# Two of every eight pairs of K tiles in the up projection by seven block products, in groups of 1024 columns

## The reference

```python
D_MODEL = 2048
D_FF = 4 * D_MODEL
...
hn = rmsnorm(h, mlp_norm[l])
u = jnp.square(jax.nn.relu(hn @ w_up[l]))
h = h + u @ w_down[l]
...
return rmsnorm(h, final_norm)
```

## Time and profile before

| what | value |
|---|---|
| median of 3 runs | 1278.83 us (1278.75 to 1278.84) |
| span of the profiled execution | 1278.0 us |
| PE busy | 1269.1 us, 99% of the span |
| DVE busy | 763.0 us, 60% |
| ACT busy | 597.0 us, 47% |
| granted TensorE clock, mean | 0.999 of 2.4 GHz |

### The profile page before, as it was taken

How to read it: one execution, slowest core, us unless ns; L and a number is a source line. 1 busy time by engine, 2 the same in 40 slices (tenths; PEclk the granted TensorE clock), 3 DMA queues, 4 the chain that set the end, 5 groups by cost and what they waited for, 6 DMA issues and landing times.

```text
span 1278.0 us, 14326 instructions
## 1 busy us (share of the span) xinstructions
PE 1269.1 (99%) x5666; PEld 1053.4 (82%) x5666; DVE 763.0 (60%) x767; ACT 597.0 (47%) x690; POOL 137.6 (11%) x239
## 2 busy tenths in 40 slices
PE   9999999999999999999999999999999999999997
PEld 7888888888888888888888888888888888888886
DVE  6676566646676677566665655444455656554544
ACT  6655345444555444444454544333344444453443
POOL 0122001103221111110111110000000101100000
PEclk9999999999999999999999999999999999999999
DMA  9698856756887688787778686555667777856563
GB/s 334 245 296 276 259 180 212 232 184 198 252 281 213 203 293 281 231 252 231 248 229 265 216 261 199 196 193 192 194 221 235 235 247 232 287 171 215 196 193 120
DMA packets 83139, 293.88 MB, mean 230 GB/s; under 512 B 11320, under 2 KB 12416, under 8 KB 82432
## 3 DMA queue, kind: packets, MB, share of 16 engines
q1 hardware_dynamic: 67536, 243.04, 57.9%
q0 software_dynamic: 14528, 48.00, 12.9%
q10 hardware_dynamic: 1008, 1.92, 0.4%
HBM read 269.45 MB, written 23.47 MB: 229 GB/s over the span
## 4 chain that ended last, share of the span: by engine, by line
PE 94%; DMA 2%; DVE 1%; POOL 1%; ACT 1%; issue 1%; DVEq 0%; POOLq 0%; ACTq 0%
PE bank L604 91%; DMA turn_rows<-blocks 1%; DMA kn<-turn_rows 1%; DVE hl L1044 1%; DMA turned_h<-turn_rows 1%; PE bank L705 1%; PE bank L687 0%; PE bank L685 0%; POOL query_rows L523 0%; PE bank L729 0%; PE bank L708 0%; POOL query_rows L522 0%; DVE blocks L1179 0%; POOL rope_t L521 0%; ACT gate L869 0%
## 5 line engine op out<-in xcount | busy, mean ns | idle before, releaser
L1044 DVE TENSOR_TENSOR hl<-raw,hl 128x1024 fp32r<-128x1024 f32 x451 | 550.3, 1230 | 467.1 <-ACT hl L824 466.7
L824 ACT ACTIVATE hl<-raw 128x1024 fp32r<-128x1024 f32 x451 | 475.4, 1059 | 599.2 <-PE bank L604 564.7
L604 PE MATMUL bank<-hl,hn_hl 128*128 128x512 f32 x1536 | 348.5, 389 | 0.0
L604 PE MATMUL bank<-hl,u_hl 128*128 128x512 f32 x1536 | 348.5, 389 | 0.0
L604 PE MATMUL bank<-hl,x_hl 128*128 128x512 f32 (+1 forms) x1536 | 345.3, 386 | 0.0
L604 PEld LDWEIGHTS bank<-hl,hn_hl 128*128 128x128 f32 x1536 | 288.3, 188 | 59.9
L604 PEld LDWEIGHTS bank<-hl,u_hl 128*128 128x128 f32 x1536 | 288.3, 188 | 59.9
L604 PEld LDWEIGHTS bank<-hl,x_hl 128*128 128x128 f32 x1536 | 283.9, 188 | 57.4 <-DVE hl L1035 0.7
L604 PE MATMUL bank<-hl,m_hl 128*128 128x512 f32 x384 | 87.2, 389 | 0.0
L604 PEld LDWEIGHTS bank<-hl,m_hl 128*128 128x128 f32 x384 | 72.1, 188 | 15.0
L500 POOL DMA_DIRECT2D turn_rows<-blocks x35 | 19.7, 562 | 555.2 <-DVE blocks L1179 554.2
(11 more groups left out here) (152 smaller groups left out, 451.8 us busy)
## 6 DMA issues: line engine op xcount, KB each, us to landing
raw<-weights SPq DMA_DIRECT2D x454, 512.0 KB, 4.3
turn_rows<-blocks POOLq DMA_DIRECT2D x34, 512.0 KB, 3.6
turned<-turn_rows POOLq DMA_DIRECT2D x96, 128.0 KB, 5.2
prob_rows<-prob_blocks POOLq DMA_DIRECT2D x8, 384.0 KB, 2.8
prob_t<-prob_rows POOLq DMA_DIRECT2D x32, 96.0 KB, 5.8
turned_h<-turn_rows POOLq DMA_DIRECT2D x20, 128.0 KB, 5.1
x_rows<-x_n POOLq DMA_DIRECT2D x2, 1024.0 KB, 8.3
resid<-x_n POOLq DMA_DIRECT2D x1, 2048.0 KB, 10.7
```

What stands on the lines that cost most here:

```text
L604: return nc.tensor.matmul(bank[:, gr.pair + tb, 0:gr.cols], tile[:, k, x_part, tb * P:tb * P + P], w, start=k == 0 and not x_part and not ...
L824: nc.scalar.activation(hl[:, slot, 0], raw[:, slot], ACT.Copy).then_inc(unit_hi, 1)
L1044: nc.vector.tensor_tensor(hl[:, slot, 1], raw[:, slot], hl[:, slot, 0].bitcast(F32), ALU.subtract).then_inc(unit_split, 1)
```

## The change

A group of up is now 1024 columns wide and uses banks 0 to 3 (bank 2c+b for column half c and token block b). A unit is one K tile of 1024 columns, still 12 matmuls. A group is 16 units, and there are 4 groups in each part. `side_by_side` is no longer used for up.

In each group the units 0, 1 and 6, 7 (`SEVEN = (0, 6)`) are taken as a pair: 2 token blocks x 2 K tiles x 2 column halves, eight block products of three passes, are replaced by seven (Winograd's form of Strassen's scheme). Four of the seven go to banks 4 to 7, where both pairs of the group add up; three go straight into banks 0 to 2. The row sums of the activations are made once per K pair, behind the return of `w_out` (`row_sums`). The sums of the weights are made for each pair on DVE (`weight_sums`), rounded on ACT (`weight_sums_to_hi`), with the remainder on DVE. ACT's rounding of the pair's first unit waits for them, since its right half is replaced by a sum.

The seven products are brought together on DVE (`sum_products`, `totals`), and the squared positive part is now made by ACT, out of SBUF (`hidden_squares`: Relu, then Square). The last two units of a group run bank by bank. The two halves of a group are transposed at different places (`turn_hidden`). The residual addition of the last `w_out` group stands one unit earlier.

```diff
+SEVEN = (0, 6)
...
     for part in range(MLP_PARTS):
-        if part == 0:
-            side_by_side("up0")
-        for g in range(2 if part == 0 else 0, FF_CHUNKS):
-            add(f"up{part}", g, KT)
+        for g in range(FF_DOUBLES):
+            add(f"up{part}", g, KT, 0, 1, 2 * WIDE)
...
+            due[gr.u0 + 10].append(("p1 copied", gr))
+            due[gr.u0 + 11].append(("products summed", gr))
+            due[gr.last + 2].append(("totals", gr))
+            for c in range(2):
+                piece = Chunk(gr.name, 2 * gr.g + c)
+                piece.of, piece.c = gr, c
+                due[gr.last + 3 + c].append(("hidden", piece))
+                due[gr.last + 4 + 2 * c].append(("hidden turns", piece))
+                due[gr.last + 13 + 2 * c].append(("u turned", piece))
+            continue
...
+        later = {("fq", 0): 5, ("fq", 1): 4, ("ukv_k", 0): 2, ("w_out", CHUNKS - 1): -1}.get((gr.name, gr.g), 0)
...
+                if had.name[:2] == "up":
+                    pe.wait_ge(totals_done, 3 * had.n + (2 if gr.pair == 0 else 3))
...
+            def three_passes(to, rows, w, first, last):
+
+                nc.tensor.matmul(bank[:, to], rows(0), w(0), start=first, stop=False)
+                nc.tensor.matmul(bank[:, to], rows(0), w(1), start=False, stop=False)
+                return nc.tensor.matmul(bank[:, to], rows(1), w(0), start=False, stop=last)
...
+                def seven_products(k):
+
+                    n, one = SUMS[k], SUMS[k] == 0
+                    last = n == len(SEVEN) - 1
+                    sum_rows = lambda i: lambda part: sums_hl[:, n, i, part]
+                    sum_weights = lambda i: lambda part: (wsum_lo if part else wsum_hi)[:, i]
+                    if gr.n == 0:
+                        pe.wait_ge(sums_split, n + 1)
+                    if one:
+                        pe.wait_ge(products_summed, gr.n)
+                    pe.wait_ge(wsum_split, 2 * SEVEN_AT[gr.u0 + k] + 1)
+                    three_passes(7, sum_rows(2), sum_weights(1), one, last)
+                    three_passes(5, sum_rows(0), sum_weights(0), one, last)
+                    pe.wait_ge(wsum_split, 2 * SEVEN_AT[gr.u0 + k] + 2)
+                    three_passes(6, sum_rows(1), sum_weights(2), one, last)
+                    pe.wait_ge(unit_split, gr.unit[k] + 1)
+                    three_passes(4, rows(k, 0), weights(k, 0), one, last).then_inc(seven_summed, 1)
+                    if one:
+                        if gr.before.name == "w_out":
+                            pe.wait_ge(resid_done, RESID0["w_out"] + gr.before.g + 1)
+                        elif gr.before.name[:2] == "up":
+                            pe.wait_ge(totals_done, 3 * gr.before.n + 2)
+                        else:
+                            pe.wait_ge(resid_done, RESID0[gr.before.name] + gr.before.g + 1)
+                    three_passes(1, rows(k + 1, 1), weights(k, 1), one, False).then_inc(unit_used, 1)
+                    pe.wait_ge(unit_split, gr.unit[k + 1] + 1)
+                    three_passes(0, rows(k + 1, 0), weights(k + 1, 1), one, False)
+                    if one:
+                        if gr.before_right.name[:2] == "up":
+                            pe.wait_ge(totals_done, 3 * gr.before_right.n + 3)
+                        else:
+                            pe.wait_ge(resid_done, RESID0[gr.before_right.name] + gr.before_right.g + 1)
+                    three_passes(2, sum_rows(3), weights(k + 1, 0), one, False).then_inc(unit_used, 1)
...
+                BANKS = [(0, 0), (1, 0), (0, 1), (1, 1)]
+                k = 0
+                while k < gr.units - 2:
+                    before_unit(k)
+                    if k in SUMS:
+                        seven_products(k)
+                        k += 2
+                        continue
+                    pe.wait_ge(unit_split, gr.unit[k] + 1)
+                    for tb, c in BANKS:
+                        done = three_passes(2 * c + tb, rows(k, tb), weights(k, c), (k, tb, c) == (2, 1, 1), False)
+                    done.then_inc(unit_used, 1)
+                    k += 1
+                before_unit(k)
+                for tb, c in BANKS:
+                    for i in range(k, gr.units):
+                        pe.wait_ge(unit_split, gr.unit[i] + 1)
+                        done = three_passes(2 * c + tb, rows(i, tb), weights(i, c), False, i == gr.units - 1)
+                    if c == 0:
+                        done.then_inc(block_left, 1)
+                done.then_inc(unit_used, 2)
...
+            def weight_sums_to_hi(n):
+
+                act.wait_ge(wsum_pair, n + 1)
+                nc.scalar.activation(wsum_hi[:, 0:2], wsum[:, 0:2], ACT.Copy).then_inc(wsum_rounded, 1)
+                act.wait_ge(wsum_done, n + 1)
+                nc.scalar.activation(wsum_hi[:, 2], wsum[:, 2], ACT.Copy).then_inc(wsum_rounded, 1)
...
-            def positive_part(gr):
-
-                act.wait_ge(unit_used, gr.last + 1)
-                act.wait_ge(blocks_turned, TURN_NO[gr.name, gr.g])
-                nc.scalar.activation(full[:], bank[:, gr.pair:gr.pair + 2], ACT.Relu).then_inc(positive, 1)
+            def copy_p1(gr):
+
+                act.wait_ge(seven_summed, len(SEVEN) * (gr.n + 1))
+                if gr.n:
+                    act.wait_ge(blocks_turned, TURN_NO["up0", 0] + 2 * gr.n)
+                nc.scalar.activation(hid[:, 1], bank[:, 4], ACT.Copy).then_inc(p1_copied, 1)
+
+            def hidden_squares(piece):
+
+                d, c = piece.of.n, piece.c
+                act.wait_ge(totals_done, 3 * d + 2 + c)
+                z = hid[:, 1 + 2 * c:3 + 2 * c]
+                nc.scalar.activation(z, z, ACT.Relu).then_inc(positive, 1)
+                act.wait_ge(positive, 2 * d + c + 1)
+                nc.scalar.activation(z, z, ACT.Square).then_inc(hidden, 1)
...
+            def weight_sums(u):
+
+                n, a, b = SEVEN_AT[u], slot_of(u), slot_of(u + 1)
+                dve.wait_ge(unit_loaded[a], (u // RING + 1) * 16)
+                dve.wait_ge(unit_loaded[b], (u // RING + 1) * 16)
+                if n:
+                    dve.wait_ge(seven_summed, n)
+                nc.vector.tensor_tensor(wsum[:, 0:2], raw[:, a, WIDE:].unsqueeze(1).broadcast_to([P, 2, WIDE]),
+                                        raw[:, a:b + 1, 0:WIDE], ALU.add).then_inc(wsum_pair, 1)
+                dve.wait_ge(wsum_pair, n + 1)
+                then_wait(nc.vector.tensor_tensor(wsum[:, 2], wsum[:, 0], raw[:, b, 0:WIDE], ALU.add))
+                nc.vector.tensor_tensor(raw[:, a, WIDE:], wsum[:, 2], raw[:, b, WIDE:], ALU.add).then_inc(wsum_done, 1)
+                for i, c in enumerate((slice(0, 2), slice(2, 3))):
+                    dve.wait_ge(wsum_rounded, 2 * n + i + 1)
+                    nc.vector.tensor_tensor(wsum_lo[:, c], wsum[:, c], wsum_hi[:, c].bitcast(F32),
+                                            ALU.subtract).then_inc(wsum_split, 1)
...
+            def sum_products(gr):
+
+                dve.wait_ge(p1_copied, gr.n + 1)
+                then_wait(nc.vector.tensor_tensor(hid[:, 0], bank[:, 6], hid[:, 1], ALU.subtract))
+                then_wait(nc.vector.tensor_tensor(hid[:, 2], hid[:, 0], bank[:, 7], ALU.add))
+                nc.vector.tensor_tensor(hid[:, 3:5], hid[:, 0:3:2],
+                                        bank[:, 5].unsqueeze(1).broadcast_to([P, 2, WIDE]),
+                                        ALU.add).then_inc(products_summed, 1)
+
+            def totals(gr):
+
+                dve.wait_ge(products_summed, gr.n + 1)
+                dve.wait_ge(block_left, 2 * gr.n + 1)
+                nc.vector.tensor_tensor(hid[:, 1], bank[:, 0], hid[:, 1], ALU.add).then_inc(totals_done, 1)
+                dve.wait_ge(block_left, 2 * gr.n + 2)
+                nc.vector.tensor_tensor(hid[:, 2], bank[:, 1], hid[:, 2], ALU.subtract).then_inc(totals_done, 1)
+                dve.wait_ge(unit_used, gr.last + 1)
+                nc.vector.tensor_tensor(hid[:, 3:5], bank[:, 2:4], hid[:, 3:5], ALU.add).then_inc(totals_done, 1)
+
+            def turn_hidden(piece):
+
+                dve.wait_ge(hidden, 2 * piece.of.n + piece.c + 1)
+                turn_blocks(piece, hid[:, 1 + 2 * piece.c:3 + 2 * piece.c])
+                if (piece.name, piece.g) == ("up0", 1):
+                    square_rms()
...
-                    dve.wait_ge(positive, HIDDEN0[gr.name] + gr.g + 1)
-                    nc.vector.tensor_tensor(full[:], full[:], both, ALU.mult).then_inc(token_out, 1)
-                    dve.wait_ge(token_out, gr.n + 1)
-                    turn_blocks(gr, full[:])
-                    if gr.name == "up0" and gr.g == 1:
-                        square_rms()
```

(33 more changed lines are left out.)

82 lines of the change are left out of this document (67 added, 15 removed).

## The result

The changed kernel takes 1294.04 us (four runs, 1288.84 to 1295.21) against 1278.84: ratio 1.0108, interval 1.0087 to 1.0130. It is 1.1% slower. The forecast was 1277.7, the range ended at 1287.0. The profiled execution is the fastest of the four (1288.84, span 1287.0), so its trace shows 9.0 us of the loss; the first two experiments bear on the other 5.

What follows compares the result with a forecast made beforehand. PE was taken to bound the kernel, busy 99% of the span without gaps in up. Terms -10.9 + 6.2 + 2.6 + 1.0 = -1.1 us gave span 1276.9, median 1277.7 us; range 1272.0 to 1287.0.

Steps and rivals of the forecast that it cites:

- PE's work: In up, 16 pairs by seven products save 48 matmuls of 0.227 us: 10.9 us less PE work.
- The rival on the pace: In the seven products, met waits break the matmuls' pipelining and cost 18 us: 1296 us; chance 6%.
- Durations on DVE and ACT: Instruction times taken for up: sums of 1024 columns 1.23 us, of 512 0.69; Relu and Square 1.05 each.
- Up to down: At two boundaries PE waits for DVE's last totals in banks 2 and 3: 1.3 us each, 2.6 in all.
- down to up: At one boundary PE waits ahead of bank 1 for DVE's additions to `resid`: 1.0 us.
- Up to up: At six boundaries PE waits at k=6 for remainders of weight sums, behind the store and second transpose: 6.2 us.
- L: Time after PE's end of an up group until DVE has its second total: 0, growing to 2.1 us.
- the rival on the store: Store of the left half takes longer, paid at each up boundary: 9.0 us at 1.5 us longer, 1286.7; chance 21%.
- w_out to up0: Behind `w_out` the wait is covered: addition ready at about 2.0 us against 2.7; row sums done early; cost nothing.
- Clock: Rival: PE's new pauses make the clock fall, 16 pairs running at 1.2 GHz cost 76 us; chance 1%.
- Its signs: PE busy 11 us less in up; wrong if k=6 waits are absent or above 2 us, or gaps stand mid group.
- Sum: Whole kernel: -10.9 + 6.2 + 2.6 + 1.0 = -1.1 us, span 1278.0 to 1276.9.

Runs made afterwards that it cites:

- the first two experiments: The changed kernel again, unaltered: 1293.46 us; then the changed kernel with the right half transposed two units later: 1279.65 us.
- Experiment 11: Changed kernel, all pairs by eight products, later second transpose, down's bank pairs swapped, `w_out` addition a unit earlier, banks 2 and 3 first in up0: 1285.14 us.
- Experiment 3: Changed kernel with the pairs of banks swapped for down: 1288.64 us, ratio 1.0064.
- experiment 6: Changed kernel with the read-back of the turned hidden tiles cut to 32 of 1024 columns: 1283.95 us, ratio 1.0041.
- experiment 4: Changed kernel's regrouping alone: all pairs by eight products, no weight sums, no products to add up: 1294.14 us, ratio 1.0115.
- 9: Changed kernel with later second transpose, down's bank pairs swapped, and the `w_out` addition one unit earlier still: 1273.89 us, ratio 0.9960.
- 10: Changed kernel with later second transpose, swapped bank pairs, earlier `w_out` addition, and up0's first pair by eight products, banks 2 and 3 first: 1271.80 us.
- Experiment 5: Kernel before, with one wait added for PE at the start of up1, on the last addition of down0: 1284.62 us, ratio 1.0044.

## Why the prediction was wrong, point by point

- *PE's work* (-10.9): right. Experiment 11 shows 9.9 of 10.2 for 45 matmuls. The rival on the pace is out.
- *Durations on DVE and ACT:* right to 0.05 us.
- *Up to down* (2.6) and *down to up* (1.0): right, with 1.32 twice and 1.01 of idle time; with restarts 3.1 and 1.3. Experiment 3 takes them away.
- *Up to up* (6.2): measured 9.7. The mechanism held link by link. L came as forecast within 0.8, and a load that lands in 6.0 was mild: those issued at 682 to 690 took up to 8.9 us, which answers to the earlier trace rows (tile `raw` of the changed kernel):

```profile
DMA to landing us min/median/max: 3.5/7.7/8.9
```

  The mis-sized term is the store: 4.4 us from transpose to transpose was met or beaten three times, and 5.7, 5.4 and 4.9 came in the other three, 2.8 us in all, as the rival on the store said, at a third of its mildest price of 9.0. The argument against it, that a store with two loads beside it took its ordinary time, held in up of the kernel before and did not carry over; the same kernel had 4.82 elsewhere. Some 1.2 us are restarts behind five waits; the other links, some longer and some shorter, give 0.5 back. The formula of the Trainium skill ("DMA: Bandwidth & Descriptors", Anatomy of one DMA) that gave 3.2 us beside the 6.0 stands there for transfers that GpSimd issues; these loads are SyncE's. Where the reads are cut, in experiment 6, L does stay at 1.0 and below.
- *w_out to up0* (nothing): wrong, 4.6 us. The step "ready at about 2.0 against 2.7" counted DVE's work from the boundary on and took the sums ahead of it as done in time. They were held up by a load, and the addition stands behind them. The row sums were indeed free. Experiments 4, 9 and 10 show that it is the queue, not the place of the addition.
- *Clock* (1%, priced as all or nothing at 76 us): the step that failed as an idea. It does not fall for a stage; it falls for five to eleven matmuls behind a pause, in some executions, at 0.2 us for each, 1.3 to 1.6 us in all and once 2.5 (experiment 4). This is 4.8 of the 5.6 us between the two profiled executions, and about half of the 5 us between the first and the median. Experiment 5 shows it by itself, in the kernel before. The page "TensorE: Matmul & The Clock Gate" of the Trainium skill had been weighed for bank cycling alone, and no run shows a fall from it: the granted clock is 1.00 in every stretch of up of the first profile above, where the seven cycle through the banks.
- *Its signs:* the waits stand where it said and on what it said, and DVE is busy for 10 us more in each 42. But two waits at k=6 are above 2 us (2.74 and 2.11) and a gap of 0.20 stands in the middle of a group (653.03), both of which it had named as signs of being wrong. PE is busy for 6.7 us less and not 11, because busy time counts a matmul next to a pause at its whole length.
- *Sum:* -1.1 forecast. +4.6, +3.5, +0.5, +0.3 and 2.0 of breaks too short to be priced make +9.8 between `w_out` and down1; with -1.0 ahead and +0.2 behind that is the 9.0 of the trace. Of the median's other 5 the clock is about half; what the rest is, no trace shows.

What is open: why a store or a load is slow at one boundary and not at the next; the runs show that the two go with stores, reads and loads issued together, not which of them delays which; one store was slow even with the reads cut (6). Nor is it shown what makes the clock fall behind a pause in one execution and hold in another.

## What to carry to other kernels

Where work is added to an engine that runs in order, do not ask whether its busy time fits, but what stands directly ahead of each instruction that the critical engine waits for, and move anything that waits for a DMA behind it: one number in the table was worth 14 us here. Price every new pause of TensorE above its length, by some 0.25 us for the restart and, for one of some 2 us and more, by 1.3 to 1.6 us for the clock in part of the executions (once 2.5). And when a term is costed at nothing, its inputs need the same bounds as the terms that carry the sum.

## What had not been expected of the hardware

A single pause of 1.8 to 3.8 us between dense matmuls can be followed, within 1.6 us of PE's restart, by five to eleven matmuls at 0.43 us instead of 0.227. A pause of 3.25 was so followed in one profile of the same program and not in the other. Of the 19 pauses of 1.8 us and more between `w_out` and down1 in all profiles here, nine were followed so (the shortest 1.83 us), and ten were not (the longest 3.28); none of the shorter ones was. Loads of 512 KB freed together behind reads landed in up to 8.9 us, against 3.4 in quiet. A wait that is met too late, even by nearly nothing, costs PE 0.1 to 0.3 us.
